# First output projection in 512+256-column products, norm weights applied on ScalarE, residual and closing products over groups of tiles

## The reference, cut to what matters

```python
def rmsnorm(x, g):
    return x * lax.rsqrt(jnp.mean(x * x, axis=-1, keepdims=True) + NORM_EPS) * g

# first_block
y = merged @ w_out                      # out1
x = x + gt_m * rmsnorm(y, g[1])         # residual sum behind out1
h = rmsnorm(x, g[2]) * (1.0 + sc_f) + sh_f
y = swiglu_ffn(h, w_ffn_in, w_ffn_out)  # ffa, ffb, down1
x = x + gt_f * rmsnorm(y, g[3])         # residual sum behind down1
# second_block
...
x = x + (silu(h2 @ w_ffn_gate) * (h2 @ w_ffn_up)) @ w_ffn_down   # ff2, down2
return rms_norm(x, final_norm_w)        # closing products
```

## Time and profile before

| | |
|---|---|
| runs of the kernel before | 3464.55, 3465.98, 3467.57 us; median 3465.98 |
| profiled execution | 3464.15 us, span 3462.1 us |
| granted PE clock, mean | 0.982 |
| PE busy | 3298.3 us (95%) |
| PEld busy | 2990.0 us (86%) |
| DVE busy | 2393.5 us (69%) |
| ACT busy | 1494.9 us (43%) |
| POOL busy | 454.6 us (13%) |
| phase out1 (PE on merged_split) | 895.5 to 986.3 us |

### The profile page before, as it was taken

One profiled execution on the slowest core, in us unless ns is written; L12 is line 12 of the kernel. 1 busy time (PEld: TensorE's weight loads), 2 busy tenths in 40 slices (PEclk: granted clock), 3 DMA queues, 4 the chain that ended last, 5 costly groups with the idle time before them and its releaser, 6 DMA issues.

```text
span 3462.1 us, 53479 instructions
## 1 busy us (share of the span) xinstructions
PE 3298.3 (95%) x20912; PEld 2990.0 (86%) x20912; DVE 2393.5 (69%) x2467; ACT 1494.9 (43%) x1538; POOL 454.6 (13%) x309
## 2 busy tenths in 40 slices
PE   1799999999989999999989999999999999999998
PEld 0799999999978888888868888888888888888887
DVE  8799987777776666666676657656777766666554
ACT  1455555634444444433354444344344444444332
POOL 2065557720100000000000000000002100000000
PEclk7899999999999999999999999999999999999999
DMA  9765554567845555566734444555555555555554
GB/s 401 278 232 216 213 191 179 180 235 294 309 157 186 192 187 189 193 232 248 271 119 169 161 170 170 187 189 182 194 187 190 192 185 192 188 188 191 188 191 146
DMA packets 111026, 706.34 MB, mean 204 GB/s; under 512 B 13376, under 2 KB 24256, under 8 KB 30672
## 3 DMA queue, kind: packets, MB, share of 16 engines
q1 hardware_dynamic: 100416, 693.86, 54.8%
q10 hardware_dynamic: 10512, 11.11, 1.0%
HBM read 702.83 MB, written 2.10 MB: 204 GB/s over the span
## 4 chain that ended last, share of the span: by engine, by line
PE 82%; DVE 8%; issue 4%; ACT 3%; POOL 2%; DMA 1%; DVEq 0%; ACTq 0%; POOLq 0%; SPq 0%
PE acc L523 44%; PE acc L524 23%; PE acc L520 4%; PE acc L522 4%; PE acc L521 4%; DVE ring_lo L1307 2%; DVE ring_raw L1329 1%; ACT ring_hi L859 1%; POOL s_w L1985 1%; PE p_norm L569 1%; POOL s_x L1987 0%; PE p_y L587 0%; POOL s_x L1984 0%; PE p_z L597 0%; DVE qk_sin L1557 0%
## 5 line engine op out<-in xcount | busy, mean ns | idle before, releaser
L1307 DVE TENSOR_TENSOR ring_lo<-ring_raw,ring_hi 128x2048 fp32r<-128x2048 f32 (+1 forms) x576 | 1311.7, 2279 | 571.4 <-ACT ring_hi L859 570.3
L523 PE MATMUL acc<-h_split,ring_hi 128*128 128x512 f32 x4736 | 1655.5, 392 | 9.2 <-DVE h_split L1369 4.5
L524 PE MATMUL acc<-h_split,ring_lo 128*128 128x256 f32 x4736 | 1337.5, 282 | 0.0
L859 ACT ACTIVATE ring_hi<-ring_raw 128x2048 fp32r<-128x2048 f32 (+1 forms) x576 | 1070.8, 1862 | 410.1 <-DMA ring_raw<-w_down 153.4
L523 PEld LDWEIGHTS acc<-h_split,ring_hi 128*128 128x128 f32 x4736 | 891.7, 188 | 197.3 <-issue 9.7
L524 PEld LDWEIGHTS acc<-h_split,ring_lo 128*128 128x128 f32 x4736 | 897.7, 190 | 0.4
L523 PE MATMUL acc<-ffn_split,ring_hi 128*128 128x512 f32 x1408 | 488.2, 390 | 0.0
L520 PE MATMUL acc<-h_split,ring_hi 128*128 128x256 f32 x1408 | 404.3, 287 | 77.5 <-DVE h_split L1369 67.3
L1926 POOL TENSOR_TENSOR sq_sum<-sq_sum,tile 128x256 f32<-128x256 f32 x60 | 76.4, 1274 | 2571.9 <-ACT tile L885 2571.9
L524 PE MATMUL acc<-ffn_split,ring_lo 128*128 128x256 f32 x1408 | 397.1, 282 | 0.0
L522 PE MATMUL acc<-h_split,ring_lo 128*128 128x256 f32 x1408 | 396.4, 282 | 0.0
(11 more groups left out here) (342 smaller groups left out, 3824.7 us busy)
## 6 DMA issues: line engine op xcount, KB each, us to landing
ring_raw<-w_ff SPq DMA_DIRECT2D x88, 1024.0 KB, 4.8
ring_raw<-w_down SPq DMA_DIRECT2D x64, 1024.0 KB, 4.8
ring_raw<-w_ffb SPq DMA_DIRECT2D x56, 1024.0 KB, 4.8
ring_raw<-w_heads SPq DMA_DIRECT2D x48, 1024.0 KB, 4.8
ring_raw<-w_mix SPq DMA_DIRECT2D x48, 1024.0 KB, 4.7
ring_raw<-w_ada SPq DMA_DIRECT2D x32, 1024.0 KB, 7.1
ring_raw<-w_ret SPq DMA_DIRECT2D x32, 1024.0 KB, 4.8
ring_raw<-w_glu SPq DMA_DIRECT2D x32, 1024.0 KB, 4.9
```

The source lines that it names most:

```text
L523: mm(dst[:], hi[s][:, t, :], moving[:, k, :], start=start, stop=False, skip_group_check=True)
L524: return mm(dst[:, T:], lo[s][:, t, :], moving[:, k, 0:T], start=False, stop=stop, skip_group_check=True)
L859: run(hi[s][:, 0:n, :], raw[s][:, 0:n, :], COPY).then_inc(hi_done, 1)
L1307: tt(lo[s][:, 0:n, :], raw[s][:, 0:n, :], hi[s][:, 0:n, :], SUB).then_inc(lo_done, 1)
```

## The change: what it does

- `out1` leaves the phases with `thirds`. PE issues one 512-column and one 256-column matmul for each k in place of three of 256, and its first iteration is written out. DVE now takes each tile out with `whole`, behind `split_lo`; for the very last tile it does so ahead of `split_lo`. The asides stay behind both.
- In `down`, ACT waits for DVE's `sum_done`, squares `y1[:, d, :]` from SBUF, and then multiplies the tile in place by `gain[:, 1, d]` (activation Identity with a scale), which DVE did in `residual`. It no longer copies the tile out of PSUM. In `down2` it likewise multiplies x by `gains[:, 6, d]` behind the square.
- The residual sum behind out1 is written out on DVE: for groups of 4, 4, 4, 2, 1 and 1 tiles one TENSOR_TENSOR by `rstd` (broadcast over the group) and one adding to x.
- `residual`, now used behind down1 only, loses its loop: the products stay one tile each, the sums go by the same groups, each sum waiting for its group's last product.
- The closing products are TENSOR_TENSOR by `rstd` over groups of 4, 4, 4, 2 and 2 tiles, and SP sends the same groups (five DMAs, three of 512 KB and two of 256 KB, in place of eight of 256 KB).

```diff
-    for name in ("u", "heads", "ret", "glu", "out1"):
+    for name in ("u", "heads", "ret", "glu"):
         ph[name].thirds = True
...
+        SUM_GROUPS = [(0, 4), (4, 4), (8, 4), (12, 2), (14, 1), (15, 1)]
+        OUT_GROUPS = [(0, 4), (4, 4), (8, 4), (12, 2), (14, 2)]
...
-            for kt in range(0, KT, 2):
-                sp.wait_ge(out_ready, kt + 2)
-                sp.dma_start(out[kt:kt + 2].rearrange("k p t -> p k t"), x[:, kt:kt + 2, :]).then_inc(out_sent, 16)
-            sp.wait_ge(out_sent, 16 * KT // 2)
+            for j, (k, n) in enumerate(OUT_GROUPS):
+                sp.wait_ge(out_ready, j + 1)
+                sp.dma_start(out[k:k + n].rearrange("k p t -> p k t"), x[:, k:k + n, :]).then_inc(out_sent, 16)
+            sp.wait_ge(out_sent, 16 * len(OUT_GROUPS))
...
-                for g in bodies(pe, p):
+                for g in bodies(pe, p, first=p.first_out == 0):
...
-                            if p.thirds:
-                                product_done(p, g, m)
-                                square_of(stage, acc[o % 2][:, 0:T], d, o % 2)
-                                evac(p, g, o, m, y[:, d, :])
+                            if updates is None:
+                                evacuated(p, g, o)
                             else:
-                                if updates is None:
-                                    evacuated(p, g, o)
...
+                                act.wait_ge(y_done, d + (16 * updates + 1))
+                            square_of(stage, y[:, d, :], d, o % 2)
+                            if blocks == 1 and updates is None:
+                                run(y[:, d, :], y[:, d, :], ACT.Identity, scale=gain[:, 1, one(d)]).then_inc(y_scaled, 1)
+                            elif updates == 3:
+                                run(x[:, d, :], x[:, d, :], ACT.Identity, scale=gains[:, 6, one(d)]).then_inc(x_scaled, 1)
+                            elif updates == 2:
...
             def residual(y, i, stds):
                 inverse_std(stds)
-                with dve.Fori(0, KT // 4) as q:
...
+                for j, (k0, n) in enumerate(SUM_GROUPS):
+                    for k in range(k0, k0 + n):
+                        ins = stt(y[:, k, :], y[:, k, :], gain[:, i, k:k + 1], rstd[:], MUL, MUL)
+                    ins.then_inc(y_times, 1)
+                    dve.wait_ge(y_times, len(SUM_GROUPS) + j + 1)
+                    at = slice(k0, k0 + n)
+                    tt(x[:, at, :], x[:, at, :], y[:, at, :], ADD).then_inc(y_done, n)
...
-            for g in bodies(dve, p):
+            for g in bodies(dve, p, last=1):
                 own.enter(1, g)
                 for o in range(4):
+                    if isinstance(g, int) and o == 3:
+                        whole(p, g, o, o, y1[:, 4 * g + o, :])
                     ahead(p, g, o)
+                    if not (isinstance(g, int) and o == 3):
+                        whole(p, g, o, o, y1[:, 4 * g + o, :])
                     if o % 2 == 0:
                         ada_aside("out1", g, o // 2, 2 * g + (4 * KT + 8))
...
-            residual(y1, 1, 2)
+            inverse_std(2)
+            for j, (k, n) in enumerate(SUM_GROUPS):
+                at = slice(k, k + n)
+                dve.wait_ge(y_scaled, k + n)
+                tt(y1[:, at, :], y1[:, at, :], rstd[:].unsqueeze(1).to_broadcast([P, n, T]), MUL).then_inc(y_times, 1)
+                dve.wait_ge(y_times, j + 1)
+                tt(x[:, at, :], x[:, at, :], y1[:, at, :], ADD).then_inc(y_done, n)
...
             inverse_std(7)
-            for kt in range(KT):
-                stt(x[:, kt, :], x[:, kt, :], gains[:, 6, kt:kt + 1], rstd[:], MUL, MUL).then_inc(out_ready, 1)
+            for k, n in OUT_GROUPS:
+                dve.wait_ge(x_scaled, k + n)
+                tt(x[:, k:k + n, :], x[:, k:k + n, :], rstd[:].unsqueeze(1).to_broadcast([P, n, T]), MUL).then_inc(out_ready, 1)
```

More of the change, by code:

```diff
@@ L416, in program @@
         t0_done, mt_done, mx_done, mx_hi, mx_split = (sem(n) for n in ("t0_done", "mt_done", "mx_done", "mx_hi", "mx_split"))
-        y_done = sem("y_done")
+        y_done, y_scaled, x_scaled, y_times = sem("y_done"), sem("y_scaled"), sem("x_scaled"), sem("y_times")
         out_ready, out_sent = sem("out_ready"), sem("out_sent")
@@ L1111, in down @@
                             d = 4 * g + o
-                            if p.thirds:
-                                product_done(p, g, m)
-                                square_of(stage, acc[o % 2][:, 0:T], d, o % 2)
-                                evac(p, g, o, m, y[:, d, :])
-                            else:
-                                if updates is None:
-                                    evacuated(p, g, o)
[L1119 to L1123, removed]
+                            if updates is None:
+                                evacuated(p, g, o)
+                            else:
+                                act.wait_ge(y_done, d + (16 * updates + 1))
[5 more added lines that the diff above has]
+                            elif updates == 2:
+                                run(h[:, d, 0:T], x[:, d, :], ACT.Identity, scale=gains[:, 5, one(d)]).then_inc(n_hi, 1)
             def ffn(p, pair0, dst, first, a, b, t, stage=None):
@@ L1649, in _ @@
             p = ph["out1"]
-            for g in bodies(dve, p):
+            for g in bodies(dve, p, last=1):
                 own.enter(1, g)
                 for o in range(4):
+                    if isinstance(g, int) and o == 3:
+                        whole(p, g, o, o, y1[:, 4 * g + o, :])
                     ahead(p, g, o)
+                    if not (isinstance(g, int) and o == 3):
+                        whole(p, g, o, o, y1[:, 4 * g + o, :])
                     if o % 2 == 0:
                         ada_aside("out1", g, o // 2, 2 * g + (4 * KT + 8))
-                own.leave(p.iters)
+                own.leave(1 if isinstance(g, int) else p.iters - 1)
             one_plus(2, 2, 4 * KT)
             dve.wait_ge(x_in, 2 * 16)
-            residual(y1, 1, 2)
+            inverse_std(2)
[5 more added lines that the diff above has]
+                tt(x[:, at, :], x[:, at, :], y1[:, at, :], ADD).then_inc(y_done, n)
             split_lo(ph["ffa"], 0, 2)
```

## The result

| | before | after |
|---|---|---|
| median of 11 runs each, same chip | 3467.39 us (3463.90 to 3470.22) | 3473.55 us (3469.89 to 3475.58) |
| ratio to before, 95% interval | | 1.0018 [1.0010, 1.0026] |
| profiled execution | 3464.15 us | 3474.68 us |
| mean granted PE clock | 0.982 | 0.980 |

The change makes the kernel 6.2 us slower (3.5 to 9.0 by the interval). The forecast was +4.5 for the kernel and 3470.5 us for the median, where 3473.55 was measured. Of the 3.05 us between the two, 1.4 lie in the kernel before, whose median over 11 runs is 3467.39 and not the 3465.98 of the three runs shown, and 1.7 in the change.

What follows compares the result with a forecast made beforehand. PE, holding 82% of the chain that ended last, was taken as the bound. Terms +4.1 (out1's end), 0, +0.4 (behind down1) and 0 (close) gave +4.5 us on 3464.15: 3468.7, median 3470.5, range 3464 to 3476.

Steps and rivals of the forecast that it cites:

- The ring: In out1 DVE and ACT wait for each other: 5.67 us a tile, above PE's 5.55, starting 4.3 us behind.
- The reciprocal: End of out1: last reduction 3 us after PE finishes, reciprocal at 992.3 against 988.23, +4.1 us; bounds -0.2 and +5.4.
- PE's gain from the wider form: Out1's products in two matmuls instead of three: 1.6 us gained at down1's pace, 0.6 at out2's.
- rival 1: Out1: DVE and ACT's mutual waits do not bind, the last reduction follows PE directly; +0.2 us, 3466.2; chance 0.15.
- The fourth rival: PE in out1: 512+256 columns run at out2's 0.351 us, not down1's 0.347; nothing changes in the sum; no chance given.
- The residual behind out1: From the reciprocal to ACT's first square 4.31 us against 4.32 today: 0 us, between -0.35 and +0.3.
- behind down1: Residual there: first sum waits for four products, 4.76 us from the reciprocal's start; +0.4 us, between 0 and +0.6.
- The close: Final products and output DMAs: DVE 1.7 us shorter, but the path is the DMAs; 0 taken, +0.35 to -1.4.
- Rival 2: Out1: POOL's adds cost DVE 0.55 us on 7 even tiles, +3.9, 8.4 in all, 3474.4; chance 0.17.
- Rival 3: Longer PE idle time at the norms brings one or two more half-speed stretches: 3472 to 3474; chance 0.10.

## Why the prediction was right, and where it was off

**The ring: right.** 5.67 us a tile was worked out from five starts in another phase and one distance in a third; 5.67 was measured on odd tiles, 5.75 and 5.83 on even ones, where 0 and 0.15 more had been put. The first reduction was put 5.39 behind m and came at 5.38; the last was put at 88.87 and came at 89.12. The short waits of PE are there (0.1 to 0.4 us on six tiles). That the ring and its lag are the cause of the larger part is shown from two sides, by taking the scaling step out of the ring (scaling on DVE) and by changing the order (reduction first): they give 3.2 and 3.0 us back at the reciprocal. The other 1.3 to 1.5 us is the way of the last tile over DVE, which stays without the ring: 3.5 to 3.6 us from PE's last start to the reciprocal in these two kernels, 2.17 before.

**The reciprocal: +4.1 put, +4.48 measured.** Of the missing 0.4, 0.25 is the reduction's own lateness and 0.14 is the clock: the last tile's two sums on PE took 1.22 us at half speed (995.69), so the reciprocal came 3.15 behind the reduction and not 3.01. In the two kernels just named these sums ran at full speed, and it is 3.0 again.

**PE's gain from the wider form: mis-sized, without effect on the sum.** I gave the form 1.6 us over out1 (0.6 at the other row). With no ring in the way it gained nothing in two executions (85.62 in both, as before) and 1.07 in two others (84.55, 84.56), while the old form gains 3.2 by itself in some executions. This made rival 1 too cheap: its -0.2 at the reciprocal took the 1.6 us for granted, and with the ring gone +1.3 and +1.45 were measured. The fourth rival, that the change does not do on PE what it says, thus held in substance (5.65 or 5.58 us a tile, where down1's row gave 5.55 and out2's 5.62). "The ring hides the difference" stayed true, so the forecast did not move.

**The residual behind out1: 0 put, +0.22 measured, and behind down1 +0.4 put, +0.67 measured.** The same two gaps were taken too short in both. I took 0.04 us from the end of DVE's products to the sum that waits for them; it was 0.11 (999.34 + 1.22 to 1000.67, 1759.81 + 1.67 to 1761.59). And I took 0.04 from the end of DVE's sum to ACT's square. The rows of before had that at 0.21: the first sum starts at 991.92 and takes 0.415, and the square starts at 992.55. After, it is 0.19 and 0.20 (1000.67 + 1.23 to 1002.09, 1761.59 + 1.23 to 1763.02). So here a change of engine cost about 0.1 us more than a wait of DVE for itself. The later 12.24 against 12.49 is the clock once more, 5.0 against 4.0 us of the sums at half speed, times 0.29.

**The close: 0 put, +0.26 measured.** The bound of +0.35 was the right side: the first DMA started 3.04 behind the reciprocal in place of 2.70, exactly as worked out, and the DMAs did not follow DVE's faster pace (340 against 330 GB/s). The rate in this stretch is the DMAs' own.

**Rival 2, POOL's adds, fell.** The adds do meet the asides, and POOL pays for it: 2.10 to 2.18 us on a tile with an aside and 0.74 on one without, while each aside keeps its 2.28. In the reduction-first kernel the order is turned round: the add has waited for the low half, goes ahead of the aside, and the aside takes 2.83. That is the rule of the Trainium skill ("SBUF — State Buffer", Who interferes with whom), the earlier instruction blocks the later one, in both directions. The rival needed the waiting add to reach into the low half, and it does not: it ends 0.06 before it (912.05 + 2.10 against 914.21).

**Rival 3, the clock, came in small.** Half speed lasted twice as long behind out1 (13.7 against 6.8 us), as feared, but 8.7 us of it lay ahead of the sums of x, where PE mostly waits: 0.14 + 0.25 us.

**The sum.** +4.5 put, +5.7 by the intervals, +6.2 [3.5, 9.0] by the medians. Apart from the -0.15 behind down1 the small terms all erred on the same side: handovers and waits taken too short, none too long.

## What to carry to other kernels

Two engines that wait for each other once a tile form a ring: add up the start-to-start distances around it before adding an operation to either, and look at the start as well, because a ring slower than the engine it feeds keeps its opening lag to the end, where it lands on the critical path (3.0 of the 4.5 us here). What is then moved away from the end gives little back while the ring is late. And when sums are grouped, the first waits for the whole first group and the last for the whole last one; the gain of fewer instructions was on an engine that was not the bound.

## What the runs showed of the hardware

- The same program, at a granted clock of 1.00 throughout, issued its 256-column matmuls 113 to 114 ns apart in one execution and 117 to 119 ns in another, from the wait at the opening of out1 to its end: 3.2 us over 16 products. Of six profiled executions with the three-matmul form two had the quick pace there, and in all six the k steps ahead of that wait had the other one. The wider form has two paces too: in the changed kernel PE's products without a wait take 5.64 to 5.66 us up to its first wait for DVE, and 5.58 or 5.66 behind later ones. So the pace can change when PE waits. It is not set by how long PE waited at the opening (0.4 to 1.8 us in the slow ones, 0.6 and 1.5 in the quick ones), and in four of six executions with the wider form the opening wait left it as it was. What sets it stays open, and it is as large as half the effect under study.
- Half-speed stretches lasted 3.4, 6.8, 10.2 or 13.7 us, and their length behind the same norm differed between executions of the same program (6.8 and 10.2 behind down1, kernel before).
- Grouping products and sums over four tiles takes DVE 2.47 us for four tiles as two TENSOR_TENSOR (999.34 to 1001.81), 2.92 with four products of 256 columns and one sum (1759.81 to 1762.73).
